# A hybrid decoder step on one core: sample queries computed ahead, pieces of the prompt redistributed over the groups, and a second buffer for transposed probabilities

## The chip, the cores and the metric

One core of one Trainium2 chip runs the kernel. The metric is the device time of one execution in microseconds. A core has these engines: TensorE (PE: matmuls and transposes by a matmul with the identity), VectorE (DVE), ScalarE (ACT), GpSimd (POOL) and SyncE (SP), which only issues DMAs. SP, ACT and POOL each issue DMAs in the order of their own program.

## The reference

The kernel computes one layer of a decoder for 512 prompt tokens and for 8 sequences of 8 sample tokens that have 4096 past positions each. Per group of tokens:

```python
qa, ka, va, qb, kb, vb = _project(_rms_norm(x, norm_attn_g[l]), w_in[l], pos)   # w_in is 1024 x 3072
oa = diff_attention(qa, ka, va, lam)       # 4 heads, 2 components of 64, values of 128; paged cache for the samples
ob = dilated_attention(qb, kb, vb)         # 8 heads of 64, windows 128/512/2048 with strides 1/4/16
x = x + _merge_heads(oa, ob, subln_g[l], w_out[l], lambda_init)
x = x + _swiglu(_rms_norm(x, norm_ffn_g[l]), w_gate[l], w_up[l], w_down[l])     # 2816 wide
```

A final norm follows. The samples' attention reads all past keys and values: 256 pages of 128 positions for the first kind of heads, and the last 2048 positions of each sequence for the second. The new keys and values, and the window buffers moved on by 8 positions, are outputs too. Everything is float32.

## The kernel before, in words

The kernel is written out by hand, one program per engine, with semaphores. Two things run interleaved: the prompt's work and the samples' attention.

**Groups.** The samples' attention is cut into 8 items (`QUADS`: four with 8 groups of pages, four with 3), 44 groups in all (`KSLOTS`). The main loop runs over `SLOTS` = 53 slots `t` with eight steps `i` each. In slot `t` the keys of group `t` are loaded (8 DMAs of 256 KB), transposed on VectorE (`turn_page`, L2280), multiplied with the samples' queries on TensorE (`score_keys`, L1305, half at step 2 and half at step 6) and moved out of PSUM with a running maximum (`keep_scores`, L2317). In the same slot the values of group `t - LAG` (`LAG` = 8) are weighed: `turn_probs` transposes the probabilities into PSUM bank X (L1318), ScalarE's `evac_probs` copies them to `pt_sb` (L1800, L1804), and `weigh_values` multiplies them with the values (L1342, L1359). The first 8 slots have keys alone, slots 8 to 43 keys and values, slots 44 to 52 values alone. `pt_sb` is one tile, so `evac_probs` waits until the group before has been weighed. In the last slots the values come from the samples' window state, and the DMAs for half of them are issued by ScalarE right behind `evac_probs`.

**Queries.** `fetch_q` and `fetch_first_q` lay an item's queries out for the scores. The first item needs the samples' columns of the first four tiles of the projection, after rotation (`rope`, L2154 to L2158).

**Pieces.** The prompt's work up to the feed-forward part is a list of 316 pieces: 192 of the projection (24 tiles of `w_in`, eight pieces a tile, six matmuls a piece, over all 576 columns, prompt and samples together), then prompt attention (32 units of one head and 128 queries, two pieces a unit), the output projection from piece 266 on, and the second norm of the prompt from piece 303 on. Each product of the projection is made of three fp32r matmuls: the weights and the activations are split into a high and a low part (`split_hi` on ScalarE L1594, `split` on GpSimd L1006, `norm_lo` on VectorE L2134). `SHARE` says how many pieces each slot takes; the 36 pieces of `PRE` run ahead of slot 0. Every engine goes through its part of each piece at the same place of its program, so the order is the same on all.

```python
PRE = 36
SHARE = [6] * 8 + [8] * 14 + [5] * 20 + [4, 4] + [3] * 4 + [0] * (SLOTS - 48)
```

**Start.** SP loads the prompt rows (blocks 0 to 3) and the sample rows (block 4), the gain, the first three tiles of `w_in` and constants, and then waits for the constants before it loads the first keys. The five blocks are normed in the order 0 to 4, transposed on TensorE (L1094) and split; the projection starts when all ten low halves are there. The move of the key window of sequence 0 (four DMAs of about 1 MB, `shift_window`, L780) runs beside the first tiles; the other moves run in the feed-forward part.

**End.** After slot 52 come the samples' output projection (`sample_out`, L1381), whose second half needs the last item's output, and the feed-forward part. Its gate and up products (L1410) and the down projection (L1477) keep TensorE busy to the end.

## Time and profile before

| | us |
|---|---|
| three runs | 1069.75, 1073.51, 1060.89; median 1069.75 |
| the profiled execution | 1071.72 |
| its span (first to last instruction) | 1070.0 |
| TensorE busy | 948.3 (89% of the span) |
| VectorE busy | 667.0 (62%) |
| ScalarE busy | 516.6 (48%) |
| GpSimd busy | 287.7 (27%) |
| DMA moved | 310.99 MB, 291 GB/s over the span |

The stages in the trace, with the end of a slot taken as the end of its `keep_scores`: norm of the input to 25.6 us; the 36 pieces ahead of the slots to about 60; slot 0 ends at 71.8, slot 7 at 126.3, slot 21 at 310.4, slot 23 at 334.9, slot 32 at 450.6, slot 35 at 484.4, slot 43 at 595.6; the values alone and the samples' output projection to 665.1; then the feed-forward part.

Busy time is not the bound by itself. A matmul's row in the trace lasts longer than the distance to the next row, since they are pipelined, and a busy share over the whole span mixes stages with different limits. The granted clock says how fast TensorE could run in a stretch; it has two levels, 1.2 and 2.4 GHz, shown as 0.5 and 1.0, and a stretch with both shows a number between them. DMA share is the mean busy share of 16 engines; a share of 1 or a little more means that they were always occupied.

### The profile page before, as it was taken

What the parts mean: (1) busy time and instruction counts of PE and PEld (TensorE: products, weight loads), DVE (VectorE), ACT (ScalarE), POOL (GpSimd) and SP (SyncE); (2) the same over time, 40 slices, a digit from 0 to 9 for tenths busy, and PEclk for the clock granted to TensorE, in tenths of its full rate; (3) what the DMA queues carried; (4) which work ended last, traced back from release to release, by engine and by line L of the source; (5) the groups of instructions that cost most, each with busy time, mean ns of one, the idle gap of its engine ahead of it and who ended that gap; (6) DMA issues with size and microseconds to landing.
All of it is one profiled execution on the core that took longest, in us unless ns stands there. A gap on an engine that the chain in (4) does not pass through costs nothing.

```text
span 1070.0 us, 29358 instructions
## 1 busy us (share of the span) xinstructions
PE 948.3 (89%) x11042; PEld 844.3 (79%) x11042; DVE 667.0 (62%) x1632; ACT 516.6 (48%) x1128; POOL 287.7 (27%) x351
## 2 busy tenths in 40 slices
PE   3989999899977888888898568899999999999996
PEld 2978888788855656676676444899999999999996
DVE  5289845676569997863546355888888888700004
ACT  6554433375236468664242653555555555611124
POOL 1322155555433355335454000000000000233330
PEclk8989999999999999998999868999999999999998
DMA  7789999999999999899988974487686876974632
GB/s 227 270 293 327 350 321 378 365 369 374 381 366 385 370 382 347 275 337 337 357 268 265 304 217 161 162 309 279 243 317 261 310 276 233 338 252 161 230 140 89
DMA packets 158229, 310.99 MB, mean 291 GB/s; under 512 B 14049, under 2 KB 88162, under 8 KB 157090
## 3 DMA queue, kind: packets, MB, share of 16 engines
q1 hardware_dynamic: 134242, 233.92, 63.0%
q0 software_dynamic: 22144, 72.37, 19.1%
q10 hardware_dynamic: 1728, 3.15, 0.9%
q8 instruction: 74, 1.21, 0.5%
q14 instruction: 41, 0.34, 0.1%
HBM read 302.31 MB, written 73.92 MB: 352 GB/s over the span
## 4 chain that ended last, share of the span: by engine, by line
PE 38%; issue 32%; DMA 15%; DVE 6%; ACT 5%; POOL 2%; POOLq 1%; ACTq 0%; SPq 0%; DVEq 0%
DMA v_ring<-in_cache_v_diff 12%; PE ps L1477 11%; PE ps L1111 9%; PE ps L1342 5%; PE ps L1305 4%; PE ps L1262 2%; DVE kt_sb L2280 1%; DMA v_ring<-in_state_v_win 1%; ACT rot L1616 1%; POOL v_ring L698 1%; PE ps L1318 1%; PE ps L1359 1%; PE ps L1188 1%; DMA x<-in_x_prompt 1%; DMA k_ring<-in_cache_k_diff 1%
## 5 line engine op out<-in xcount | busy, mean ns | idle before, releaser
L2280 DVE STREAM_TRANSPOSE kt_sb<-k_ring 128x512 f32<-128x512 f32 x336 | 218.7, 688 | 67.7 <-DMA k_ring<-in_cache_k_diff 30.7
L698 POOL DMA_DIRECT2D v_ring<-in_cache_v_diff x248 | 136.3, 551 | 157.6 <-issue 84.5
L1050 POOL TENSOR_TENSOR c_lo<-c_raw,c_hi 128x1408 fp32r<-128x1408 f32 x14 | 46.6, 3331 | 410.7 <-ACT c_hi L1893 410.7
L1111 PE MATMUL ps<-h_hi,w_hi 128*128 128x288 f32 x384 | 124.8, 325 | 1.9 <-DVE h_lo L2134 1.9
L1111 PE MATMUL ps<-h_lo,w_hi 128*128 128x288 f32 x384 | 115.8, 301 | 0.0
L1342 PE MATMUL ps<-v_ring,pt_sb 128*32 128x128 f32 x2240 | 79.2, 283 | 40.8 <-DMA v_ring<-in_cache_v_diff 34.0
L1111 PE MATMUL ps<-h_hi,w_lo 128*128 128x288 f32 x384 | 115.3, 300 | 0.0
L1342 PEld LDWEIGHTS ps<-v_ring,pt_sb 128*32 128x32 f32 x2240 | 61.1, 113 | 53.2 <-issue 49.5
L1305 PE MATMUL ps<-kt_sb,q_st 128*32 128x128 f32 (+1 forms) x2816 | 95.4, 278 | 6.2 <-DVE q_st L2290 4.1
L1006 POOL TENSOR_TENSOR w_lo<-w_raw,w_hi 128x1024 fp32r<-128x1024 f32 x24 | 57.4, 2392 | 153.7 <-ACT w_hi L1594 153.7
L1305 PEld LDWEIGHTS ps<-kt_sb,q_st 128*32 128x32 f32 x2816 | 72.0, 113 | 23.1 <-issue 16.2
L1111 PEld LDWEIGHTS ps<-h_hi,w_hi 128*128 128x128 f32 x384 | 74.5, 194 | 15.9 <-issue 13.6
L1477 PE MATMUL ps<-a_hi,c_hi 128*128 128x288 f32 x352 | 79.1, 296 | 0.2 <-POOL c_lo L1050 0.2
L1410 PE MATMUL ps<-t_h,s_h 128*128 128x288 f32 x264 | 77.9, 295 | 1.1 <-ACT u L1886 1.1
L1477 PE MATMUL ps<-a_lo,c_hi 128*128 128x288 f32 x352 | 78.9, 295 | 0.0
L1477 PE MATMUL ps<-a_hi,c_lo 128*128 128x288 f32 x352 | 78.5, 294 | 0.0
L1410 PE MATMUL ps<-t_l,s_h 128*128 128x288 f32 x264 | 77.9, 295 | 0.0
L1410 PE MATMUL ps<-t_h,s_l 128*128 128x288 f32 x264 | 77.7, 294 | 0.0
L2419 DVE TENSOR_TENSOR s_l<-s_t,s_h 128x512 fp32r<-128x512 f32 x88 | 58.7, 687 | 28.5 <-ACT s_h L1857 18.1
L1111 PEld LDWEIGHTS ps<-h_lo,w_hi 128*128 128x128 f32 x384 | 74.7, 195 | 0.0
L1111 PEld LDWEIGHTS ps<-h_hi,w_lo 128*128 128x128 f32 x384 | 74.6, 194 | 0.0
L2570 DVE TENSOR_TENSOR x<-x,ps 128x512 f32 x7 | 4.8, 686 | 111.1 <-PE ps L1490 111.1
(249 smaller groups left out, 2346.9 us busy)
## 6 DMA issues: line engine op xcount, KB each, us to landing
k_ring<-in_cache_k_diff SPq DMA_DIRECT2D x256, 256.0 KB, 7.1
v_ring<-in_cache_v_diff POOLq DMA_DIRECT2D x248, 256.0 KB, 7.0
out_k_win_sample<-in_state_k_win SPq DMA_DIRECT2D x32, 1020.0 KB, 8.2
out_v_win_sample<-in_state_v_win SPq DMA_DIRECT2D x32, 1020.0 KB, 8.2
k_ring<-in_state_k_win SPq DMA_DIRECT2D x32, 512.0 KB, 6.7
w_raw<-in_w_in SPq DMA_DIRECT2D x24, 512.0 KB, 7.3
g_raw<-in_w_gate SPq DMA_DIRECT2D x11, 1024.0 KB, 5.4
g_raw<-in_w_up SPq DMA_DIRECT2D x11, 1024.0 KB, 5.4
```

Source lines behind the costliest of these rows:

```text
L698: queue.dma_start(dst, src.rearrange("(b j) c -> j b c", b=4))\
L1006: nc.gpsimd.tensor_tensor(w_lo[:, n % 3, :], w_raw[:, n % 3, :], w_hi[:, n % 2, :].bitcast(F32), ALU.subtract).then_inc(w_lo_done, 1)
L1050: nc.gpsimd.tensor_tensor(c_lo[j][:, 0:width], c_raw[:, j, 0:width], c_hi[j][:, 0:width].bitcast(F32), ALU.subtract).then_inc(w_lo_done, 1)
L1111: last = nc.tensor.matmul(M[c][:, 0:HALF], wt, act[:, k, c * HALF:(c + 1) * HALF], start=k == 0 and at_first, stop=k == KT - 1 and act is ...
L1188: last = nc.tensor.matmul(Y[:, qb * P + 64 * c:qb * P + 64 * c + 64], weights_t, v_tok[:, kb, T * P + 64 * c:T * P + 64 * c + 64], start=k ...
L1262: last = nc.tensor.matmul(M[m % 2], wt, act[:, k, :], start=k == 0 and at_first, stop=k == KT - 1 and act is mix_h and not at_first)
L1305: last = nc.tensor.matmul(S[32 * f:32 * f + 32, c0:c0 + 32 * n], q_st[place_of(it)][:, h, f, r, :], kt_sb[:, 4 * h:4 * h + n, c:c + 32], s ...
L1342: last = nc.tensor.matmul(O[32 * f:32 * f + 32, P * h:P * h + P], pt_sb[:, 4 * f + b, :], values[:, f * P:(f + 1) * P], start=g == 0 and b ...
L1410: last = nc.tensor.matmul(ps[:, bank, 0:HALF], wt[:, k, :], act[:, k, :], start=j in (0, 1, 3) and k == 0 and at_first, stop=k == 3 and wt ...
L1477: last = nc.tensor.matmul(main_ps[:, 2 * bank + c, 0:HALF], wt[j][:, w], a_lo[:, pair, block, :] if low else a_hi[pair][:, block, :], star ...
L2280: V.transpose(kt_sb[:, i, :], k_ring[:, i, :]).then_inc(kt_done, 1)
L2419: V.tensor_tensor(dst[:, :, :], src, high[:, :, :].bitcast(F32), ALU.subtract).then_inc(form_low, 1)
```

## The change

1. **Samples' queries first.** The sample block is normed first (`NORM_ORDER`), and `project_samples` multiplies its transposed rows with the first four weight tiles in plain f32, straight from the raw weights, as soon as those land. `copy_sample_queries` and `rope_sample_queries` finish the first items' queries before the rest of the norm. The fourth weight tile has a place of its own (`early_raw`). The projection of tiles 0 to 3 then covers the 512 prompt columns alone. ScalarE issues the loads of the prompt rows, the first keys are loaded as soon as the page numbers are there, and the four moves of sequence 0's key window go to the down projection.
2. **All pieces in the groups.** `PRE` is 0. `SHARE` gives 9 pieces to each of slots 0 to 7, 8 to slots 8 to 21 as before, 6 or 5 (once 7) to slots 22 to 35, 5 and 5 to 36 and 37, and 4 to slots 38 to 47. The fourth item's queries are laid out in place 0 at the end of slot 23, where they came into place 1 in steps during it.
3. **Two places for transposed probabilities.** From slot 44 on `pt_sb` has two tiles, and from slot 45 on `turn_probs` and `evac_probs` of a slot run at step 5 of the slot before.

The core of the diff:

```diff
-    return 0 if it < 3 else it % 2
-
-
-FETCH_AT = {23: 3, 30: 4, 33: 5, 36: 6, 39: 7}
+    return 0 if it < 4 else (it + 1) % 2
+
+
+FETCH_AT = {30: 4, 33: 5, 36: 6, 39: 7}
...
-PRE = 36
+PRE = 0
...
-SHARE = [6] * 8 + [8] * 14 + [5] * 20 + [4, 4] + [3] * 4 + [0] * (SLOTS - 48)
+SHARE = ([9] * 8 + [8] * 14 + [6] * 4 + [5] + [6] * 5 + [7] + [5, 5, 6] + [5, 5] + [4] * 10
+         + [0] * (SLOTS - 48))
...
-            if i == 4 and has_v(t):
+            if i == 4 and has_v(t) and t <= KSLOTS:
                 out.append(("p", t))
+            if i == 5 and t >= KSLOTS and has_v(t + 1):
+                out.append(("p", t + 1))
...
+def prob_place(t):
+
+
+    return t % 2 if t >= KSLOTS else 0
...
+        pt_sb = [at("pt_sb0", [P, 16, 32], region(2048)), at("pt_sb1", [P, 16, 32], W0 + 28672)]
...
+        NORM_ORDER = (4, 0, 1, 2, 3)
...
+            return slice(256 * c, 256 * c + 256) if n < 4 else slice(c * HALF, (c + 1) * HALF)
...
-                if n >= 3:
+                if n >= 4:
                     sp.wait_ge(w_used, n - 2)
...
+            load_x(4)
+            sp.dma_start(g_rows[:, :], ins["norm_attn_g"].partition_broadcast(P)).then_inc(norm_in[0], 16)
+            sp.dma_start(ident[:, :], consts[:, C_ID:C_ID + P]).then_inc(norm_in[0], 16)
+            sp.dma_start(page_ids[:, :], ins["page_table"].rearrange("b n -> (b n)").unsqueeze(0)).then_inc(norm_in[0], 16)
+            for n in range(4):
+                w_in_chunk(n)
...
+            sp.wait_ge(norm_in[0], 48)
+            for i in range(8):
+                load_keys(0, i)
...
-
-            sp.wait_ge(const_in, 16 * N_CONST)
-            for i in range(8):
-                load_keys(0, i)
...
-                    if j == 0 and n and n + 2 < TILES:
+                    if j == 0 and n >= 2 and n + 2 < TILES:
...
-                    if j == 4 and n < COPIES:
-                        shift_window(*shifts.pop(0))
...
+                if m % 2:
+                    shift_window("k_win", 0, m // 2)
...
                 if j == 7:
                     last.then_inc(w_used, 1)
+
+            def project_samples(n):
+
+                pe.wait_ge(*landing_of(n))
+                pe.wait_ge(qs_copied, 2)
+                for k in range(KT):
+                    last = nc.tensor.matmul(Z[1][:, n * NS:n * NS + NS], raw_at(n)[:, k * P:k * P + P], h_s[:, k, :],
+                                            start=k == 0, stop=k == KT - 1)
+                last.then_inc(qs_projected, 1)
 
             def turn_tokens(n):
...
+            norm_transposes(0, NORM_ORDER[0])
+            for n in range(4):
+                project_samples(n)
+            for u in range(1, NBLK):
+                norm_transposes(u, NORM_ORDER[u])
             pe.wait_ge(hlo_done, 2 * NBLK)
-            for p in range(PRE):
-                main(p)
...
+            def copy_sample_queries():
+
+                act.wait_ge(qs_projected, 4)
+                cols = slice(0, 4 * NS)
+                nc.scalar.activation(feat[:, 1, cols], Z[1][:, cols], ACT.Copy).then_inc(qs_copied, 1)
+                act.wait_ge(qs_copied, 3)
+                for q in range(4):
+                    s = slice(32 * q, 32 * q + 32)
+                    d = slice(32 * (q ^ 1), 32 * (q ^ 1) + 32)
+                    last = nc.scalar.activation(rot[d, cols], feat[s, 1, cols], ACT.Copy)
+                last.then_inc(qs_copied, 1)
...
-                if q:
+                pt = pt_sb[prob_place(t)]
+                if t > KSLOTS:
+                    act.wait_ge(pv_half[1], q - 1)
+                    act.wait_ge(pv_half[0], q - 1)
+                elif q:
                     act.wait_ge(pv_half[1], q)
...
-                if t > KSLOTS and has_v(t + 2):
-                    place_state(act, q + 2, 1)
+                if t > KSLOTS + 1 and has_v(t + 1):
+                    place_state(act, q + 1, 1)
...
+                if u >= 2:
+                    act.wait_ge(sumsq_done, u - 1)
+                norm_stats(u, NORM_ORDER[u])
+
+            for blk in range(4):
+                act.dma_start(x[0:P, blk, :], x_of(blk)).then_inc(x_in[blk], 16)
+            squares_of(0)
+            norm_root(0, NORM_ORDER[0])
+            act.wait_ge(xn_t, 1)
+            for q in range(2):
+                nc.scalar.activation(h_s[:, 4 * q:4 * q + 4, :],
+                                     norm_bank(0, 4, q).rearrange("p (k c) -> p k c", k=4)[:, :, 0:NS], ACT.Copy)\
+                    .then_inc(qs_copied, 1)
+            norm_hi(0, NORM_ORDER[0], h_hi)
             split_hi(0)
-            for blk in range(NBLK):
-                norm_hi(blk, blk, h_hi)
+            squares_of(1)
+            norm_root(1, NORM_ORDER[1])
+            squares_of(2)
+            norm_root(2, NORM_ORDER[2])
+            copy_sample_queries()
+            squares_of(3)
+            norm_root(3, NORM_ORDER[3])
+            norm_hi(1, NORM_ORDER[1], h_hi)
+            fetch_q(0)
+            squares_of(4)
+            norm_root(4, NORM_ORDER[4])
+            norm_hi(2, NORM_ORDER[2], h_hi)
+            norm_hi(3, NORM_ORDER[3], h_hi)
+            norm_hi(4, NORM_ORDER[4], h_hi)
             act.wait_ge(lam_step, 2)
             nc.scalar.activation(lam_exp, lam_sum, ACT.Exp).then_inc(lam_e, 1)
-            for p in range(PRE):
-                main(p)
...
+            def rope_sample_queries():
+
+                dve.wait_ge(const_in, 16 * N_CONST)
+                dve.wait_ge(qs_copied, 4)
+                for f in range(4):
+                    s = slice(f * NS, f * NS + NS)
+                    V.tensor_tensor(feat[:, 1, s], feat[:, 1, s], rope_cs[:, 0, SEQ:NT], ALU.mult)
+                    last = V.tensor_tensor(rot[:, s], rot[:, s], rope_cs[:, 1, SEQ:NT], ALU.mult)
+                last.then_inc(rope_parts, 2)
+                dve.wait_ge(rope_parts, 2)
+                for f in range(4):
+                    s = slice(f * NS, f * NS + NS)
+                    V.tensor_tensor(q_s[:, f, :], feat[:, 1, s], rot[:, s], ALU.add).then_inc(rope_s_done, 1)
+
             def norm_blocks():
-                for blk in range(NBLK):
-                    norm_mean(blk, blk)
-                    if blk:
-                        norm_rows(blk - 1, blk - 1)
-                norm_lo(0, 0, h_hi, h_lo)
-                norm_rows(NBLK - 1, NBLK - 1)
-                for blk in range(1, NBLK):
-                    norm_lo(blk, blk, h_hi, h_lo)
+                def mean(u):
+                    norm_mean(u, NORM_ORDER[u])
+
+                def rows(u):
+                    norm_rows(u, NORM_ORDER[u])
+
+                def low(u):
+                    norm_lo(u, NORM_ORDER[u], h_hi, h_lo)
+
+                mean(0)
+                dve.wait_ge(norm_in[0], 48)
+                rows(0)
+                low(0)
+                mean(1)
+                rows(1)
+                mean(2)
+                rows(2)
+                rope_sample_queries()
+                fetch_first_q()
+                mean(3)
+                low(1)
+                rows(3)
+                mean(4)
+                low(2)
+                rows(4)
+                low(3)
+                low(4)
...
+                c = slice(0, SEQ if n < 4 else NT)
+                V.tensor_tensor(feat[:, n % 2, c], feat[:, n % 2, c], rope_cs[:, 0, c], ALU.mult).then_inc(rope_parts, 1)
+                V.tensor_tensor(rot[:, c], rot[:, c], rope_cs[:, 1, c], ALU.mult).then_inc(rope_parts, 1)
+                dve.wait_ge(rope_parts, 2 * no + 2)
+                if n >= 4:
+                    V.tensor_tensor(dst_s[:, T, :], feat[:, n % 2, SEQ:NT], rot[:, SEQ:NT], ALU.add).then_inc(rope_s_done, 1)
                 V.tensor_tensor(dst[:, T, :], feat[:, n % 2, 0:SEQ], rot[:, 0:SEQ], ALU.add).then_inc(rope_done, 1)
```

How the order moves, at three places. First VectorE in the norm of the input, before the change; `h_lo` are the low halves of the prompt and sample columns, `q_s` the rotated sample queries, `xn` the normed rows:

```order
L2134 TENSOR_TENSOR h_lo<-ps,h_hi 128x4x128 x2
L2107 RECIPROCAL small<-small 64x1
L2117 SCALAR_TENSOR_TENSOR xn<-x,small,g_rows 64x1024
L2134 TENSOR_TENSOR h_lo<-ps,h_hi 128x4x128 x6
L2134 TENSOR_TENSOR h_lo<-ps,h_hi 128x4x64 x2
L2481 TENSOR_TENSOR lam_prod<-lam_in 128x128
L2483 TENSOR_REDUCE small<-lam_prod 128x2
```

The same engine with the change, from the third block's rows on:

```order
L2221 TENSOR_TENSOR feat<-feat,rope_cs 128x64
L2222 TENSOR_TENSOR rot<-rot,rope_cs 128x64
L2227 TENSOR_TENSOR q_s<-feat,rot 128x64 x4
L2403 COPY q_st_125<-q_s 32x8x8 x8
L2180 TENSOR_SCALAR small<-small 128x1
L2212 TENSOR_TENSOR h_lo<-ps,h_hi 128x4x128 x2
L2185 RECIPROCAL small<-small 128x1
L2195 SCALAR_TENSOR_TENSOR xn<-x,small,g_rows 128x1024
```

The sample queries' rotation and the layout of the first item's queries (L2221 to L2403) now stand ahead of two blocks' rows and of all eight low halves of the prompt, for which the projection waits.

TensorE at its start, before the change; `ps` is PSUM, `h_hi` and `h_lo` the split activations:

```order
L1094 MATMUL ps<-ident,xn 128x128 x32
L1094 MATMUL ps<-ident,xn 128x64 x8
L1111 MATMUL ps<-h_hi,w_hi 128x288
L1111 MATMUL ps<-h_lo,w_hi 128x288
L1111 MATMUL ps<-h_hi,w_lo 128x288
```

And with the change:

```order
L1118 MATMUL ps<-ident,xn 128x64 x8
L1148 MATMUL ps<-h_s,w_raw 128x64 x24
L1148 MATMUL ps<-h_s,early_raw 128x64 x8
L1118 MATMUL ps<-ident,xn 128x128 x32
L1136 MATMUL ps<-h_hi,w_hi 128x256
```

The 32 plain f32 matmuls of the samples stand between the sample block's transposes and those of the prompt, and the first pieces of the projection have 256 columns where they had 288.

TensorE in slots 45 to 48, before the change; `t_ring`, `k_ring` and `v_ring` hold values here, and `ident,s_sb` are transposes of probabilities:

```order
L1373 MATMUL ps<-v_s,ptm 32x128 x8
L1094 MATMUL ps<-ident,xn_110 128x128 x8
L1318 MATMUL ps<-ident,s_sb 128x128 x4
L1342 MATMUL ps<-t_ring,pt_sb 32x128 x16
L1419 MATMUL ps<-ident,o_row 128x128
L1342 MATMUL ps<-t_ring,pt_sb 32x128 x16
L1094 MATMUL ps<-ident,xn_110 128x128 x8
L1318 MATMUL ps<-ident,s_sb 128x128 x4
L1342 MATMUL ps<-k_ring,pt_sb 32x128 x32
L1318 MATMUL ps<-ident,s_sb 128x128 x2
L1359 MATMUL ps<-v_ring,pt_sb 32x128 x32
L1326 MATMUL ps<-ident,s_sb 64x128
```

And with the change:

```order
L1407 MATMUL ps<-v_s,ptm 32x128 x8
L1118 MATMUL ps<-ident,xn_111 128x128 x8
L1352 MATMUL ps<-ident,s_sb 128x128 x4
L1376 MATMUL ps<-t_ring,pt_sb_67 32x128 x16
L1453 MATMUL ps<-ident,o_row 128x128
L1118 MATMUL ps<-ident,xn_111 128x128 x8
L1376 MATMUL ps<-t_ring,pt_sb_67 32x128 x16
L1118 MATMUL ps<-ident,xn_111 128x128 x8
L1352 MATMUL ps<-ident,s_sb 128x128 x2
L1376 MATMUL ps<-k_ring,pt_sb_68 32x128 x32
L1352 MATMUL ps<-ident,s_sb 128x128 x4
L1393 MATMUL ps<-v_ring,pt_sb_67 32x128 x32
```

The transposes of a slot's probabilities (L1318, now L1352) now stand ahead of the weighing of the slot before, and the `pt_sb` tiles alternate. The rest of the prompt's norm transposes (L1094, now L1118) still stands between them.

## Rows read from the trace of the kernel before

**Rows 1.** Windows: length, then PE, PEld, DVE, ACT, POOL busy us, clock, DMA share, GB/s.

```profile
0.00:25.60 25.60, 7.33 (x40) 6.61 (x40) 13.50 (x26) 15.49 (x29) 4.04 (x8) 0.91 0.78 222
25.60:60.00 34.40, 33.92 (x234) 33.68 (x234) 12.43 (x27) 20.04 (x32) 11.96 (x5) 0.91 0.75 258
60.00:71.80 11.80, 8.12 (x90) 7.41 (x91) 7.84 (x26) 6.74 (x16) 2.40 (x1) 0.71 0.91 315
71.80:126.30 54.50, 53.22 (x734) 47.98 (x733) 49.53 (x130) 22.08 (x39) 11.96 (x5) 1.00 1.03 341
126.30:310.40 184.10, 170.43 (x2578) 147.98 (x2579) 108.17 (x291) 82.78 (x180) 86.04 (x118) 0.98 1.03 364
334.90:450.60 115.70, 96.88 (x1607) 72.60 (x1608) 98.60 (x348) 76.12 (x234) 49.65 (x90) 0.99 0.98 350
484.40:595.60 111.20, 95.46 (x1338) 72.52 (x1333) 52.07 (x168) 34.65 (x107) 51.18 (x71) 0.92 0.96 308
595.60:665.10 69.50, 46.25 (x690) 31.22 (x689) 33.04 (x76) 40.50 (x75) 0.00 (x0) 0.78 0.67 199
665.10:1070.00 404.90, 391.13 (x2954) 389.66 (x2952) 245.07 (x384) 181.75 (x310) 46.63 (x14) 0.99 0.66 243
```

**Rows 2.** Timeline 23 to 66 us: start, duration, engine, operation [idle before].

```profile
23.47 4.57 SPq L830 DMA_DIRECT2D k_ring<-in_cache_k_diff  x8
25.63 0.61 PE L1111 MATMUL ps<-h_hi,w_hi 128*128 128x288 f32 x1 [1.88 <-DVE h_lo L2134]
60.18 2.11 ACT L1783 ACTIVATE q_st<-q_s 32x64 f32<-32x64 f32 x8 [1.45 <-DVE q_s L2157]
61.94 1.59 DVE L2290 COPY q_st<-q_s 32x64 f32<-32x64 f32 x8
...
63.67 1.93 PE L1305 MATMUL ps<-kt_sb,q_st 128*32 128x128 f32 x32 [4.13 <-DVE q_st L2290]
```

**Rows 3.** Timeline 69 to 72 us, TensorE: one half of a group, a piece.

```profile
69.68 1.08 PE L1305 MATMUL ps<-kt_sb,q_st 128*32 128x128 f32 x32
...
71.06 0.29 PE L1111 MATMUL ps<-h_hi,w_lo 128*128 128x288 f32 x1
71.19 0.29 PE L1111 MATMUL ps<-h_hi,w_hi 128*128 128x288 f32 x1
```

**Rows 4.** Groups by line and shape, 0 to 66 us: prices of the norm.

```profile
L2117 DVE SCALAR_TENSOR_TENSOR xn<-x,small,g_rows 128x1024 f32<-128x1024 f32 x4 | 5.1, 1284 | 1.0 <-PE ps L1094 0.9
L2134 DVE TENSOR_TENSOR h_lo<-ps,h_hi 128x512 fp32r<-128x512 f32 x8 | 5.0, 674 | 0.0
L1585 ACT ACTIVATE h_hi<-ps 128x512 fp32r<-128x512 f32 x8 | 4.1, 586 | 0.2 <-PE ps L1094 0.2
```

**Rows 5.** Groups by line, VectorE, 334.9 to 450.6 us: key transposes, masks.

```profile
L2280 DVE STREAM_TRANSPOSE kt_sb<-k_ring 128x512 f32<-128x512 f32 x73 | 47.9, 687 | 0.4 <-PE ps L1305 0.4
L2172 DVE CUSTOM_DVE_ANT_0 prob<-ps,p_mask 128x384 f32<-128x384 f32 (+3 forms) x44 | 19.8, 484 | 1.8 <-PE ps L1157 1.8
```

**Rows 6.** Timeline: two units of prompt attention one behind the other.

```profile
336.55 0.92 PE L1157 MATMUL ps<-kT,qT 64*128 64x384 f32 x4
340.10 1.13 PE L1157 MATMUL ps<-kT,qT 64*128 64x512 f32 x4 [0.47 <-DVE small L2172]
```

**Rows 7.** Waits, 595 to 665 us: us in total, times, longest.

```profile
PE ps L1342 <- ACT pt_sb L1800: 11.8, 4, 5.9
PE ps L1359 <- ACT pt_sb L1804: 5.4, 3, 3.1
PE ps L1373 <- ACT ptm L1817: 4.2, 3, 3.5
```

**Rows 8.** Timeline of ScalarE at 600 us: a table load and what follows.

```profile
600.62 1.28 ACT L1835 ACT_TABLE_LOAD   x1
601.91 0.51 ACT L1835 ACTIVATE s_sb<-s_sb,small 128x256 f32<-128x256 f32 x1
```

**Rows 9.** The page, sixth part: DMA issues, KB each, us to landing.

```profile
out_k_win_sample<-in_state_k_win SPq DMA_DIRECT2D x32, 1020.0 KB, 8.2
```

158 lines of the change are left out of this document (74 added, 84 removed).

## The prediction

> **What bounds the kernel now.** I read the windows by stage first, since the stages have different limits; there the reader is to compare TensorE's busy time with the length, and both with the DMA share. From 665.1 us on TensorE is busy 391 of 405 us, and nothing in the change touches that stage but four more copies. From 71.8 to 126.3 us (slots 1 to 7, keys alone) it is busy 53.2 of 54.5 us, so these slots are bound by TensorE, though the DMA share is 1.03. From 126.3 to 450.6 us the DMA engines are full (shares 1.03 and 0.98, 364 and 350 GB/s), and TensorE has room, little up to 310 (170.4 of 184.1) and more behind (96.9 of 115.7). In the last slots, 595.6 to 665.1 us, nothing is full: TensorE 46.3 of 69.5 us, ScalarE 40.5, DMA share 0.67, and the granted clock is 0.78 [rows 1]. A change can win only ahead of 665.1 us: at the start, in the slots bound by DMA by giving them more of the work, and at the end of the attention.
>
> Then the timelines at the edges of these stages. The first piece starts at 25.63 us, and behind the pieces of `PRE` TensorE waits 4.13 us for the first item's queries, which VectorE lays out until 63.5 us [rows 2]. In the last slots the waits name ScalarE's copies of transposed probabilities: 11.8, 5.4 and 4.2 us, 21.4 in all [rows 7].
>
> **The prices.** A projection matmul follows the one before after 0.13 us (71.06, 71.19), so a piece of six takes 0.79 us; half a group's scores take 1.08 us [rows 3]. Slots 1 to 7 take 54.5 / 7 = 7.8 us with six pieces each [rows 1].
>
> **The start, TensorE.** The samples come first, so the prompt's norm ends later. The first keys wait until 23.47 us for the constants [rows 2]; in the first 25.6 us the DMA engines move 222 GB/s at a share of 0.78 [rows 1]. The fourth weight tile (0.5 MB) now stands ahead of the constants, 2.4 us at that rate, less what the early issue of the prompt rows by ScalarE gives back: I take the constants at 24.5 us. The plain f32 matmuls are not in the trace. A lower bound is a projection's pitch, 0.13 us; an upper one comes from slot 0's score products, 1.93 us for 32 at half the clock [rows 2], so 0.06 each, times four since they run four side by side: 0.24 us. So 32 take 4 to 8 us, and all but the last tile's 1 to 2 us lie beside the landing of the weights. They and ScalarE's copies end before the constants do; this edit costs nothing as long as the constants are later. Then VectorE rotates the queries (12 short instructions at 1.59 / 8 = 0.2 us, 2.5 us) and lays them out (1.6 us): 28.6 us. Behind that stands a chain of two engines for the last blocks: high half of block 0 (2 x 0.59), ScalarE's layout of the queries (2.1 and two more of it, 2.6), squares of the last block (1.2), roots (0.7), high halves (1.2), low half (0.7), rows (1.3), transposes (1.1), high (1.2), low (0.7) [rows 2, 4]: 11.9 us. Squares are taken like the rows, which are as wide; roots as three short instructions, transposes as eight at 0.13 us. The first piece starts at about 40.5 us in place of 25.6, 15 us later.
>
> Against that stands what TensorE no longer does before the end of slot 7. From 25.6 to 126.3 us, 100.7 us, it did 84 pieces; now 72, 12 x 0.79 = 9.5 us less. Slot 0 from 60 on took 11.8 us at a granted clock of 0.71 for three pieces and the scores, which at full clock are 3 x 0.79 + 2.2 + 0.8 = 5.3; the wait and the slow clock behind it, 6.5 us, go. Tiles 0 to 3 have 256 columns for 288: up to 192 x 0.13 x 0.11 = 2.8 us, nothing if the weight loads set the pitch; I take 2.5. So slot 7 ends at 40.5 + 100.7 - 9.5 - 6.5 - 2.5 = 122.7 us, 4 us earlier (bounds 12 earlier and 4 later, for a start at 33 or 48 us). In slots 0 to 7 the nine pieces set the pace: 7.8 + 3 x 0.79 = 10.2 us each. VectorE's eight transposes (0.69) and a rotation lie beside them. What is late next is the second group's keys: SP loads eight pages of values ahead of them once the norm's transposes are done, which just fits into slot 0.
>
> **The copies.** Four moves of 1 MB leave the start, where they lay beside pieces bound by TensorE, for the down projection. Both places have room (shares of 0.75 and 0.66), and one takes 8.2 us [rows 1, 9]. I take nothing; if the weights of the down projection came late by them, 1 or 2 us.
>
> **The slots bound by DMA.** Slots 8 to 21 have the same pieces and bytes: nothing. The debt of 12 pieces is paid behind. Up to slot 23 the projection still runs (184 of 192 pieces done at the end of slot 21), and slots 24 to 32 take 52 pieces in place of 45 (250 pieces done for 251). These nine slots took 115.7 us, 12.9 each; VectorE was busy 98.6 us, of which key transposes 47.9 and masks 19.8 [rows 1, 5]. Less 47.9 and about 1.1 us a group for the scores' way out, its work for 45 pieces is some 40 us, 0.9 a piece; TensorE's, less 4 us a group for scores and values (estimated as twice 2 x 1.08), some 60, 1.3 a piece. Seven more make VectorE 105 and TensorE 106 of 115.7 us: they fit, on average. In the first of these slots, where a unit costs VectorE most, they fit less well, and the queries of the fourth item are now laid out in one lump (20 copies of 0.26 us, 5 us on ScalarE) between slots 23 and 24, with TensorE's scores behind. I take 3 us of loss; below, nothing; above, see the first rival.
>
> **The output projection.** Slots 38 to 41 have four pieces for five; the real work of the moved ones goes to 42 and 43, where TensorE had room (95.5 of 111.2 us busy over the eight slots [rows 1]). Four pieces of 1.3 us are 5 us; the DMA share of 0.96 lets me take 2.
>
> **The last slots.** With a probability copy made one slot ahead, TensorE finds it there. Of the 21.4 us of waits those in slot 44 and those for `ptm` stay in part, say 9; 12 go, and with them some time at the slow clock. But the copies stand on ScalarE in a row with the norm's squares and roots and the exponentials of the last item, 40.5 us of work, and the norm starts a little later, since three pieces more stand ahead of it. The order of the changed program has seven table loads there where nine stood; a load takes 1.28 us and the exponential starts 0.01 us behind it [rows 8], so 2.6 us go. The Trainium skill (ScalarE: Activation LUTs, What ACT_TABLE_LOAD costs) says that a switch costs 2.66 us, as a drain of 1.38 us belongs to it; by that two fewer would give 5.3 us. The row shows no such pause. I follow the rows: 10 us in all (bounds 3, the table loads alone, and 15). What is late next is the value DMAs, which ScalarE issues between its copies.
>
> **The sum.** 4 - 3 + 2 + 10 = 13 us. The profiled execution took 1071.7 us with a span of 1070.0; it would become 1058.7. It lies 2 us above the median of the three runs, 1069.75, so I predict 1057 us. The three runs differ by 12.6 us, and about 1% is what a measurement of this kernel tells from no change.
>
> The prompt rows now go through ScalarE's queue. The Trainium skill (DMA: Bandwidth & Descriptors, Issuing engines are not separate DMA queues) says that this saves only issue time, since all queues share the same engines. The share of 0.78 [rows 1] leaves a little room beside it; if the second queue filled it, the constants would land some 4 us earlier and the sum would be 17, by the rule it stays 13.
>
> **The rivals.**
> - *The debt isn't hidden.* Nothing in a slot bound by DMA is free if each piece ties three engines in order. Then the 12 pieces cost their own 9.5 us and some waits, 13 in place of 3, and the time is 1067. For it: TensorE waits for VectorE's masks within a unit (0.47 us [rows 6]). Against: 84% busy.
> - *The end is bound by ScalarE and the values.* The copies move, but ScalarE's row of work keeps the pace and only the table loads go: 3 us for 10, 1064. For it: 40.5 us busy, most of it in the first slots. Against: 21.4 us of waits that name just these copies [rows 7].
> - *Slower: units set the pace.* Two units follow each other after 3.55 us, and TensorE waited for the mask in between [rows 6]; a slot of 12.9 us has 2.5 units, 5.1 us each. If that, and not the DMA, is their pace, the 12 pieces are 6 units and 31 us in place of 3, less what slots 22 and 23 give back, say 4: 24 us more, 1081. It decides against the change when a unit takes over 4.3 us (12.9 / 3) in slots 24 to 32. Against it: DMA at a share of 0.98 there.
> - *Better than thought.* The norm chain overlaps more (start at 35 us), the debt is free and the end gives 14: 5 + 3 + 4 more, 1045.
>
> **How the numbers follow.** The forecast has 0.46, the debt 0.16, the end 0.14, slower 0.10, better 0.14. The forecast's own spread is 6 us to each side; some two thirds of it lie below 1059, the limit of 1%. Faster by over 1%: 0.30 of the forecast, 0.14, and a little of the rivals near it, 0.48. Slower: 0.10. Within 1%: 0.42. The range goes from 1044 to 1076: it takes in all but half of the best case and the slow one.
>
> **What would show it.** First piece at 38 to 43 us; slot 7 ends at 119 to 126; slots 1 to 7 of about 10.2 us with TensorE full; slot 23 ends some 4 us earlier than 334.9 and slot 32 some 1 us earlier than 450.6; the last slots take 58 to 62 us in place of 69.5, with a granted clock over 0.78, and the waits for `pt_sb` fall below 9 us. A first piece after 46 us, or slots 24 to 32 of more than 13.6 us on average, would make the prediction wrong.

## The result, and the profile after

The change made the kernel slower: 1094.99 us (median of four runs, 1093.27 to 1096.61) for 1068.8 (four runs, 1060.89 to 1073.51), a ratio of 1.0264 with a 95% interval of 1.0214 to 1.0314. The forecast was 1057, the range 1044 to 1076. The profiled execution has a span of 1094.8 us, the one before 1070.0.

The windows of the changed kernel by stage, cut where [rows 1] are cut (same columns: length, PE, PEld, DVE, ACT, POOL busy, clock, DMA share, GB/s):

```profile
0.00:25.60 25.60, 11.65 (x58) 11.52 (x58) 6.92 (x11) 8.55 (x16) 4.22 (x8) 1.00 0.96 297
25.60:50.00 24.40, 13.24 (x60) 12.04 (x60) 13.62 (x43) 13.59 (x32) 0.75 (x1) 0.71 0.13 43
...
131.20:322.30 191.10, 175.25 (x2601) 152.29 (x2601) 111.51 (x286) 84.41 (x179) 92.86 (x122) 0.97 0.99 345
322.30:345.30 23.00, 17.51 (x304) 14.33 (x302) 13.50 (x45) 4.87 (x13) 8.64 (x16) 1.00 1.04 386
345.30:479.40 134.10, 108.57 (x1639) 79.90 (x1641) 109.37 (x388) 85.93 (x271) 50.54 (x91) 0.94 0.88 313
479.40:516.50 37.10, 33.24 (x514) 27.45 (x513) 24.24 (x86) 25.02 (x71) 14.62 (x25) 0.91 0.93 301
516.50:624.60 108.10, 93.03 (x1358) 70.30 (x1362) 52.25 (x167) 33.67 (x106) 49.98 (x69) 0.95 0.97 312
```

Read by stage, the loss has three places. Slot 7 ends at 131.2 for 126.3 us, where the forecast had 122.7. Slots 8 to 21 take 191.1 for 184.1 us, where it had no change. Slots 24 to 32 take 134.1 for 115.7, where it had 3 us. Slots 36 to 43 gave 3.1 us and the end 4.3.

Over slots 24 to 32 the DMA share fell from 0.98 to 0.88, but that is again an average. Slots 24 to 29 and slot 32 before, then slots 24 to 29, 30, 31 and 32 of the changed kernel:

```profile
334.90:408.50 73.60, 60.60 (x1017) 44.29 (x1018) 65.95 (x230) 46.95 (x151) 31.73 (x58) 0.98 1.03 378
436.50:450.60 14.10, 11.98 (x195) 8.85 (x188) 12.64 (x47) 9.04 (x27) 4.38 (x8) 1.00 0.80 255
```

```profile
345.30:425.60 80.30, 64.91 (x1032) 46.70 (x1033) 71.71 (x250) 48.71 (x162) 32.44 (x59) 0.94 1.02 369
425.60:441.30 15.70, 11.96 (x185) 8.93 (x185) 9.84 (x38) 13.87 (x42) 6.56 (x13) 1.00 0.84 305
441.30:457.80 16.50, 13.38 (x209) 10.36 (x211) 12.51 (x46) 11.62 (x31) 4.42 (x9) 1.00 0.70 227
457.80:479.40 21.60, 18.32 (x224) 13.91 (x219) 15.30 (x59) 11.72 (x37) 7.12 (x13) 0.84 0.57 179
```

In slots 24 to 29 the DMA engines stay full; from slot 30 on they do not, and 11.7 of the 18.4 us are lost there (before, slots 30 and 31 had shares of 0.96 and 0.95). The row 25.6 to 50 is new: for 24 us the DMA engines did next to nothing (share 0.13), because the keys of the first group had landed by 27.5 us, and what SP loads behind them (eight pages of values, the second group's keys) waits for the last of the norm's transposes, which here come at 43.5.

The start, timeline of the changed kernel, for [rows 2]:

```profile
15.03 10.48 PE L1148 MATMUL ps<-h_s,w_raw 128*128 128x64 f32 x48 [0.84 <-ACT h_s L1967]
...
25.20 3.53 PEld L1148 LDWEIGHTS ps<-h_s,early_raw 128*128 128x128 f32 x16
25.30 3.62 PE L1148 MATMUL ps<-h_s,early_raw 128*128 128x64 f32 x16
...
33.11 1.59 DVE L2403 COPY q_st<-q_s 32x64 f32<-32x64 f32 x8
...
47.43 0.58 PE L1136 MATMUL ps<-h_hi,w_hi 128*128 128x256 f32 x1 [2.01 <-DVE h_lo L2212]
```

The first piece starts at 47.43 us, not 40.5. The 32 plain f32 matmuls of the samples stand in the trace as 64 rows with 64 weight loads and take 14.1 us, 0.44 each, where the forecast's upper bound was 0.24. They run at the lower clock, though the window above shows 1.00: the trace holds no clock record ahead of 32.65 us, and a stretch without a record is shown as 1.00. The rows tell it. Plain f32 products of the same form (128 x 128 weights, 64 columns) in slot 32 of the changed kernel, at a granted clock of 1.00, take 1.00 us for eight rows, which are four matmuls, so 0.25 each:

```profile
458.60 1.00 PE L1222 MATMUL ps<-v_tok,probT 128*128 128x64 f32 x8
```

Where the granted clock is at its lower level, 16 such rows take 3.51 us (452.79 in the trace of l_late2, shown below), 0.44 a matmul again.

The end, waits of TensorE from the end of slot 43 to the first gate product (624.6 to 689.8 us), for [rows 7]:

```profile
PE ps L1453 <- ACT pt_sb L1859: 4.1, 1, 4.1
PE ps L1118 <- DVE xn L2195: 3.2, 1, 3.2
PE ps L1407 <- ACT ptm L1876: 2.3, 2, 2.0
PE ps L1360 <- ACT pt_sb L1859: 2.1, 1, 2.1
PE ps L1352 <- ACT pt_sb L1859: 2.1, 1, 2.1
PE ps L1376 <- DMA k_ring<-in_state_v_win: 1.5, 1, 1.5
PE ps L1393 <- DMA v_ring<-in_state_v_win: 1.1, 1, 1.1
```

Waits for ScalarE's copies are 10.6 us for 21.4 [rows 7], so 10.8 went, as the forecast had it (12). Table loads are seven for nine. But waits for the norm and for values came in their place (5.8 us), the clock is 0.76, and the stretch is 65.2 us for 69.5.

### The profile page after: what moved, and what is told of

The parts are those of the page before. It is cut to its first block, busy times and chain, and to the rows that moved or that the text cites. A ratio compares the mean times of both kernels' runs of the same rounds, so it can differ in the third digit from the quotient of the medians.

```text
span 1094.8 us, 29510 instructions
## 1 busy us (share of the span) xinstructions
PE 968.0 (88%) x11106; PEld 860.9 (79%) x11106; DVE 674.7 (62%) x1640; ACT 515.2 (47%) x1133; POOL 289.0 (26%) x351
## 3 DMA queue, kind: packets, MB, share of 16 engines
q0 software_dynamic: 22144, 72.37, 18.7%
## 4 chain that ended last, share of the span: by engine, by line
PE 35%; issue 30%; DMA 15%; DVE 9%; ACT 6%; POOL 1%; SPq 1%; ACTq 0%; POOLq 0%; DVEq 0%
PE ps L1514 11%; PE ps L1136 7%; DMA v_ring<-in_cache_v_diff 7%; PE ps L1339 4%; DMA k_ring<-in_cache_k_diff 4%; PE ps L1376 4%; DVE kt_sb L2393 3%; DMA wo_sb<-in_w_out 2%; DMA w_raw<-in_w_in 2%; DVE prob L2285 2%; PE ps L1296 1%; PE ps L1148 1%; PE ps L1222 1%; ACT q_st L1838 1%; PE ps L1206 1%
## 5 line engine op out<-in xcount | busy, mean ns | idle before, releaser
L1136 PE MATMUL ps<-h_hi,w_hi 128*128 128x288 f32 (+1 forms) x384 | 124.3, 324 | 2.0 <-DVE h_lo L2212 2.0
L1136 PE MATMUL ps<-h_lo,w_hi 128*128 128x288 f32 (+1 forms) x384 | 114.7, 299 | 0.0
L1136 PE MATMUL ps<-h_hi,w_lo 128*128 128x288 f32 (+1 forms) x368 | 110.2, 299 | 0.0
L1376 PE MATMUL ps<-v_ring,pt_sb 128*32 128x128 f32 x2240 | 81.8, 290 | 29.0 <-DMA v_ring<-in_cache_v_diff 22.3
L1136 PEld LDWEIGHTS ps<-h_hi,w_lo 128*128 128x128 f32 x368 | 71.7, 195 | 0.0
```

What stands on the lines that cost most here:

```text
L1136: last = nc.tensor.matmul(M[c][:, 0:cols.stop - cols.start], wt, act[:, k, cols], start=k == 0 and at_first, stop=k == KT - 1 and act is h ...
L1376: last = nc.tensor.matmul(O[32 * f:32 * f + 32, P * h:P * h + P], pt_sb[prob_place(t)][:, 4 * f + b, :], values[:, f * P:(f + 1) * P], sta ...
```

## The experiments

The edits of tables are shown as the line of `SHARE` alone, without its last term of zeros. A name in the text is the kernel's label. "Without debt" means that 84 pieces are done by the end of slot 7, as before. All ratios are to the kernel before, timed beside each; they were taken at four different times, at which the median of the kernel before was 1067.6 to 1068.7.

### First: the debt and the end, each alone

**a_pre12**, the changed kernel without debt; each engine runs 12 pieces ahead of slot 0:

```diff
-PRE = 0
+PRE = 12
+SHARE = [9] * 8 + [8] * 14 + [5] * 20 + [4, 4] + [3] * 4
```

> The changed kernel, but 12 pieces run ahead of slot 0 and the table from slot 22 on is that of the kernel before, so the debt of 12 pieces is gone. Theory D (the debt is what costs behind slot 21: a unit of prompt attention more in a slot is not hidden by the DMAs): slot 7 ends 9.5 us later than in the changed kernel (12 x 0.79), about 140.7, slots 24 to 32 take about 116 us for 134.1, slots 33 to 35 about 34, and the time is 1095 + 9.5 - 21 = about 1084. Rival S (the later start itself, with DMA engines idle from 25.6 to 50 us, is carried on into the later slots): slots 24 to 32 stay above 130 us and the time is about 1104.

**b_debt**, the kernel before with the debt alone:

```diff
-SHARE = [6] * 8 + [8] * 14 + [5] * 20 + [4, 4] + [3] * 4
+SHARE = [4, 5] * 4 + [8] * 14 + [6] * 4 + [5] + [6] * 5 + [7] + [5, 5, 6] + [5, 5] + [4] * 10
```

> The kernel before, with 4 or 5 pieces (36 in all) in slots 0 to 7 for 48, and the changed kernel's table from slot 8 on: the debt alone, without anything else of the change. Theory D: slot 7 ends 9.5 us earlier than 126.3, about 117, slots 24 to 32 take 131 to 134 us for 115.7, and the time is 1069 - 9.5 + 20 = about 1079. Rival S: the debt is hidden, slots 24 to 32 take at most 119 us, and the time is about 1062.

**c_oldtail**, the changed kernel with one `pt_sb` and the transposes at step 4 in all slots, and **d_newtail**, the kernel before with two. The edit as d_newtail has it, in part; c_oldtail takes it back:

```diff
-            if i == 4 and has_v(t):
+            if i == 4 and has_v(t) and t <= KSLOTS:
                 out.append(("p", t))
+            if i == 5 and t >= KSLOTS and has_v(t + 1):
+                out.append(("p", t + 1))
```

> The changed kernel with one place for copied probabilities and the old order at the end. The stretch from the end of slot 43 to the first gate product took 69.5 us before and 65.2 after. If the two places are what gives 4.3 us, it goes back to about 69.5 and the time is 1099. If the whole 10 us of the forecast are there but are hidden by the four pieces a slot that now stand in slots 44 to 47, it takes 75 us and the time is 1105. If the place gives nothing, 1095.

> The kernel before with the changed end alone (two places, one slot ahead). By the 4.3 us seen: 1065. By the forecast's 10 us: 1059. If the gain hung on the other order of pieces: 1069, no change.

Measured: a_pre12 1075.77 us (1.0063, 1.0032 to 1.0094); b_debt 1101.34 (1.0305, 1.0263 to 1.0347); c_oldtail 1097.59 (1.0254, 1.0217 to 1.029); d_newtail 1065.03 (0.996, 0.9924 to 0.9996). In a_pre12 slot 7 ends at 135.8 us (expected 140.7) and slots 24 to 32 take 114.5, so theory D had the place right and rival S is out; the time came 8 us under the expected 1084, and 5 of these are the 12 pieces, which cost 4.6 us by slot 7 and not 9.5. In b_debt slots 24 to 32 take 134.4 us, as theory D had it, but the time is 22 us over its 1079: slot 7 ends at 121.2 us for the 117 expected, and slots 8 to 21 take 190.8 us for 184.1. These and the rest make 21 us in the profiled execution, the fastest of its four (1093.09; the others are 1098 to 1105). By the median the debt alone costs 33 us, more than the whole change, and where the other 12 us go isn't known. The changed end is worth some 2.6 us by the median either way, with intervals of 3 to 4 us to each side; in the traces the stretch from slot 43 to the first gate product is 63.1 us in d_newtail for 69.5, and in c_oldtail 68.7 for 65.2, which is the first of its three cases.

### Second: where the debt is paid, and the start alone

**f_start**: the changed kernel with `PRE` = 36 and the table before. **g_early**: without debt, none ahead of slot 0. **i_pay**: the debt paid outside slots 28 to 32. **k_phase**: the kernel before with the tile's boundaries moved.

```diff
 f_start  SHARE = [6] * 8 + [8] * 14 + [5] * 20 + [4, 4] + [3] * 4
 g_early  SHARE = [10, 11] * 4 + [8] * 14 + [5] * 20 + [4, 4] + [3] * 4
 i_pay    SHARE = [9] * 8 + [8] * 14 + [6] * 6 + [5] * 5 + [5] * 11 + [4] * 4
 k_phase  SHARE = [6, 5] * 4 + [8] * 14 + [7, 7] + [5] * 18 + [4, 4] + [3] * 4
```

> The changed kernel with the 36 pieces ahead of slot 0 and the table of the kernel before: its start (samples first, fourth weight tile early, copies in the down projection) and its end, with no debt at all. Theory: the 36 pieces start some 22 us later than 25.63 (first piece at 47.4) and the wait for the queries (4.13 us) and the clock behind it go, so slot 7 ends at about 126 + 22 - 6.5 - 2.5 = 139; the rest as before, less 2.6 us at the end: 1077. Rival: the later start is made up in the slots bound by the DMA engines, since keys and values lie in their rings already: 1067.

> The kernel before with 44 for 48 pieces in slots 0 to 7 and the four paid in slots 22 and 23 (7, 7 for 5, 5). By slot 8 the count is 80, so each slot of 8 pieces is one whole tile, as in the changed kernel (72), where before it lay half a tile off (84). Theory P (the 7 to 8 us that the changed kernel loses in slots 14 to 21 come from where the tile's boundary falls in a slot): slots 14 to 21 take about 110 us in place of 103, slots 14 and 16 are the long ones, and the time is 1068 - 3 + 7 + 1 = about 1073. Rival (it comes from the later start of the values or from the size of the debt): 103 us there, and about 1066.

> The changed kernel with its debt of 12 pieces paid elsewhere: six of them in slots 22 to 27, none in slots 28 to 32 (five pieces each, for 6, 6, 6, 6, 7), six from slot 33 on. Theory C (slots 28 to 32 are those where the DMA engines aren't full any more and each unit more costs its own 5 us): slots 28 to 32 take 66 us for 80, slots 33 to 43 some 5 us more, and the time is about 1085. Rival (the cost follows the pieces wherever they stand): slots 28 to 32 gain, but the others lose as much, and it stays at 1095.

> The changed kernel without the debt in another way: none ahead of slot 0, but 10 or 11 pieces in each of slots 0 to 7, then the table of the kernel before. Theory: 12 pieces at 0.79 us more by slot 7, the rest as without the debt: like the run with 12 pieces ahead, 1076. If pieces in these slots are cheaper than ahead of them, since VectorE's and the DMA engines' work lies beside them: 1070; if the slots of 11 pieces let the DMA engines fall behind: 1080.

Measured: f_start 1081.85 us (1.0124, 1.0062 to 1.0187); g_early 1077.55 (1.0082, 1.0052 to 1.0112); i_pay 1084.29 (1.0135, 1.0076 to 1.0194); k_phase 1074.7 (1.0068, 1.0029 to 1.0107). The start costs more than expected: slot 7 of f_start ends at 144.2, for 139 expected. The wait ahead of slot 0's scores did go, but one slot later TensorE waits 4.39 us, behind VectorE, which sat 5.43 us idle until the second group's keys landed:

```profile
76.62 1.08 PE L1340 MATMUL ps<-kt_sb,q_st 128*32 128x128 f32 x32
84.59 2.72 DVE L2398 STREAM_TRANSPOSE kt_sb<-k_ring 128x512 f32<-128x512 f32 x4 [5.43 <-DMA k_ring<-in_cache_k_diff]
88.28 1.77 PE L1340 MATMUL ps<-kt_sb,q_st 128*32 128x128 f32 x32 [4.39 <-DVE small L2435]
```

i_pay has theory C's time, in part by luck: slots 28 to 32 take 69.6 us for 80.1 (66 expected), slots 24 to 27 cost 3.5 more, and 4.6 us come from slots 8 to 21, whose program is that of the changed kernel. g_early came out at theory's 1076 and k_phase at its 1073, each within 2 us. k_phase is 6 us slower than before with four pieces moved; in its trace slot 16 takes 18.9 us for 14.0, slots 14 to 21 take 104.4, of the 110 expected only a part (the profiled execution was the fastest of its ten).

### Third: copies, a credit, the f32 matmuls, the phase in the changed kernel

**e_copies** is d_newtail with the four copies moved; **l_late2** is e_copies with one piece less in slots 31 and 32 and one more in 44 and 45; **m_short** and **j_mix** come from the changed kernel, and m_short leaves out 28 of the 32 plain f32 matmuls.

```diff
 l_late2  SHARE = [6] * 8 + [8] * 14 + [5] * 9 + [4, 4] + [5] * 9 + [4, 4] + [4, 4] + [3] * 2
 j_mix    SHARE = [9, 10] * 4 + [8] * 14 + [6] * 6 + [5] * 5 + [5] * 9 + [4, 4] + [4, 4, 3, 3]
 m_short
-                for k in range(KT):
+                for k in (0,):
...
-                                            start=k == 0, stop=k == KT - 1)
+                                            start=True, stop=True)
```

> The kernel before with the changed end and the four copies of 1 MB in the down projection. Theory: slots 1 to 7 are bound by TensorE with or without the copies, and the down projection has room: the same as with the changed end alone, 1065. Rival: the copies crowded the keys' queue at the start (slots 3, 4 and 7 differed by up to 2 us between two executions of the same code), and without them slot 7 ends 4 us earlier: 1061.

> As the kernel with the changed end and the copies moved, and slots 31 and 32 have four pieces for five, slots 44 and 45 four for three: a credit where the changed kernel took a debt. Theory C (a unit costs some 5 us in slots 28 to 32): slots 31 and 32 take 23 to 24 us for 27.8, held up by the DMA share of 0.95 and 0.80 at which they stand, the last slots 1 us more: 3 us less than the other kernel of this call, about 1062. Rival (pieces are dearer in the last slots): no change or 2 us more.

> The changed kernel with 4 of the 32 plain f32 matmuls of the samples (the first of eight steps of each tile), so the samples' queries of the first item leave out seven eighths of their sum; it shows what these matmuls cost at the start. They took 14.1 us in the trace, 0.44 each. Theory: the fourth tile lands at 25.2 us whatever they take, so only its own 3.1 us go, the transposes of the prompt's blocks start at about 25.6 for 28.7, the first piece at 44 for 47.4, and the time is 1095 - 3 = 1092. Rival (their 14 us are the delay): first piece at 36 and 1084.

> The changed kernel with 76 pieces by slot 7 (9, 10), so that a tile's boundary falls in the middle of a slot again, and 28 to 32 left at five pieces each as in the run that paid elsewhere; four pieces less of debt. Theory P (the boundary of a tile at the boundary of a slot costs some 7 us in slots 14 to 21): 103 us there; 1084 + 3 at the start - 5 - 2 = about 1080. Rival (the later start or the debt itself): 106 to 111 us there and about 1087.

Measured: e_copies 1064.33 us (0.9959, 0.9927 to 0.9992), beside 1065.03 of d_newtail, so the copies cost and give nothing that these runs can tell. m_short 1087.95 (1.0163, 1.0107 to 1.022), first piece at 38.82: the f32 matmuls delayed it by 8.6 us and the end by 7, nearer to the rival. Theory had the landing of the fourth tile wrong: it lands at 18.83 us, and its matmuls waited for those ahead of them. j_mix: slots 14 to 21 take 103.2 us as theory P had it, and its trace has no wait of TensorE for ScalarE there. Its time settles nothing: the four runs are 1082.87 (the profiled one), 1092.26, 1100.12 and 1100.41, a median of 1096.19 (1.0267, 1.0208 to 1.0325) where 1080 was expected; the two lower ones have a mean of 1087.6, which is the rival's figure. Why this kernel's runs spread so is open.

l_late2 took theory C down: with a piece less in each of the two slots it is 1077.8 us (1.0076, 1.0047 to 1.0105), 13 us slower than e_copies. Windows of slots 31 to 33, first e_copies, then l_late2:

```profile
424.10:437.80 13.70, 11.29 (x201) 9.30 (x203) 10.44 (x43) 8.89 (x27) 6.76 (x12) 1.00 0.93 327
437.80:451.90 14.10, 11.98 (x195) 8.85 (x188) 12.64 (x47) 9.04 (x27) 4.38 (x8) 1.00 0.81 254
451.90:464.20 12.30, 11.94 (x185) 9.74 (x188) 8.06 (x36) 10.55 (x35) 4.38 (x8) 1.00 1.02 297
```

```profile
426.00:442.40 16.40, 12.14 (x181) 9.34 (x184) 9.61 (x39) 6.92 (x21) 6.76 (x12) 0.79 0.81 288
442.40:462.90 20.50, 16.13 (x199) 12.15 (x192) 12.42 (x45) 8.19 (x26) 4.38 (x8) 0.75 0.62 193
462.90:478.50 15.60, 12.60 (x186) 10.05 (x187) 8.33 (x36) 12.37 (x38) 4.38 (x8) 0.89 0.71 212
```

These are nearly the times of the changed kernel, whose slots 31 and 32 take 16.5 and 21.6 us, with six and seven pieces where l_late2 has four and four and the kernel before five and five. In l_late2 the clock says that TensorE ran slow, and the timeline says after what:

```profile
433.80 0.88 PE L1178 MATMUL ps<-ident,prob 128*128 128x128 f32 x3 [2.74 <-DVE small L2316]
434.47 1.81 PE L1194 MATMUL ps<-v_tok,probT 128*128 128x64 f32 x8
436.21 1.94 PE L1348 MATMUL ps<-v_ring,pt_sb 128*32 128x128 f32 x32
...
444.53 0.61 PE L1211 MATMUL ps<-ident,oT 128*128 128x128 f32 x4
...
451.69 1.09 PE L1324 MATMUL ps<-ident,s_sb 128*128 128x128 f32 x4 [3.58 <-DVE mix_l L2272]
452.57 0.42 PE L1178 MATMUL ps<-ident,prob 128*128 128x128 f32 x1
452.79 3.51 PE L1194 MATMUL ps<-v_tok,probT 128*128 128x64 f32 x16
...
456.23 1.94 PE L1348 MATMUL ps<-v_ring,pt_sb 128*32 128x128 f32 x32
```

At 444.53 the piece that ends a head puts its output transposes into a bank that mix_l on VectorE must have read; the group's probabilities (L1324) need it at step 4, and wait 3.58 us. Behind the wait the values' products take 1.94 us for the 1.08 of full clock. In e_copies the same transposes of a head come at 449.31, behind the probabilities, and nothing waits. The changed kernel has the same kind of wait in its slot 32, shorter, and one for VectorE's row in slot 31. There the clock stays at 1.00, so slot 31 is not long for the reason that it has in l_late2:

```profile
452.89 0.41 PE L1206 MATMUL ps<-ident,prob 128*128 128x128 f32 x2 [2.17 <-DVE small L2415]
460.99 0.70 PE L1191 MATMUL ps<-kT,qT 64*128 64x256 f32 x4 [1.38 <-DVE small L2285]
468.46 0.63 PE L1352 MATMUL ps<-ident,s_sb 128*128 128x128 f32 x4 [1.90 <-DVE mix_l L2371]
```

### Fourth: the place of a piece against the samples' steps

**p_swap** moves one piece of e_copies by one slot; **u_xearly** is l_late2 with the transposes of slot 32 one step later, on TensorE and ScalarE; **r_best** is e_copies with a debt of one whole tile, paid before slot 24.

```diff
 p_swap   SHARE = [6] * 8 + [8] * 14 + [5] * 9 + [4, 6] + [5] * 9 + [4, 4] + [3] * 4
 r_best   SHARE = [5] * 8 + [8] * 12 + [10] * 2 + [7] * 2 + [5] * 18 + [4, 4] + [3] * 4
 u_xearly
-            if i == 4 and has_v(t) and t <= KSLOTS:
+            if i == (5 if t == 32 else 4) and has_v(t) and t <= KSLOTS:
```

> The kernel before with the changed end and the copies moved, and one single piece moved by one slot: slot 31 has four, slot 32 six, all others as before. Theory X (what costs is not how many pieces a slot has, but which of them stands next to the steps of the samples' work there: the item ends in slot 31, and bank X and VectorE's row of work are shared): slots 31 and 32 take 33 us or more for 27.8, the clock falls to half behind the waits, and the time is about 1070. Rival (the count decides): 28 us for both, no change, 1064.

> The kernel of l_late2 (1078), with the probabilities' transposes and their copy in slot 32 alone at step 5 in place of 4, so behind the products of the piece that stood behind them. Theory X: the wait of 3.6 us for bank X (released by VectorE's mix_l) is filled by those products, the half clock behind it goes in part, slot 32 takes 15 to 17 us for 20.5, and the time is about 1074. Rival (VectorE's and ScalarE's chain sets the pace there, TensorE's wait is only where it shows): slot 32 stays above 19 us, 1078.

> The kernel before with the changed end, the copies moved, and a debt of eight pieces, one whole tile, in slots 0 to 7 (five each) that is paid in slots 20 to 23 (10, 10, 7, 7 for 8, 8, 5, 5), ahead of the prompt's attention proper; everything from slot 24 on as before. Theory X with DMA as the bound: the phase of the tiles is kept, the eight pieces lie beside the DMAs, slot 7 ends 6.3 us earlier, slots 20 to 23 take at most 4 us more: 1064 - 6 + 3 = 1061. Rival (no piece is hidden in a slot bound by DMA): they cost their own 6.3 us there and more, 1066.

Measured: p_swap 1068.16 us (0.999, 0.9965 to 1.0016), 4 us over e_copies, with 30.7 us in slots 31 and 32 for 27.8: theory X in sign, at half its size. Its slot 31 has l_late2's four pieces and the same wait of 2.74 us, but a granted clock of 0.89 for 0.79, and takes 15.1 us for 16.4. u_xearly 1075.61 (1.0062, 1.0037 to 1.0088): slot 32 takes 16.9 us for 20.5, the wait for `mix_l` there is 1.59 us for 3.58, and the end comes 2 us earlier, as theory X had it, less than the slot gives. So this wait is the cause of most of slot 32's loss; slots 33 to 35 take 41 us in both kernels, for 33.5 in e_copies, and that part of l_late2's 13 us isn't explained. Its waits, TensorE's rows of slots 31 and 32:

```profile
430.12 0.87 PE L1178 MATMUL ps<-ident,prob 128*128 128x128 f32 x3 [2.74 <-DVE small L2316]
...
448.08 0.63 PE L1324 MATMUL ps<-ident,s_sb 128*128 128x128 f32 x4 [1.59 <-DVE mix_l L2272]
```

r_best 1062.54 (0.9962, 0.9933 to 0.9991): faster than the changed kernel, and 0.4% under the kernel before, which is within 1%. Slot 7 ends at 123.2 us, and slots 24 to 32 take 113.9, as in e_copies (114.0). It isn't told apart from e_copies (2 us, with runs of both from 1059 to 1072).

### What the traces say together

Each number is the length of a stretch in one profiled execution, in us.

| slots | before | b_debt | after | i_pay | k_phase | j_mix | f_start | g_early | r_best |
|---|---|---|---|---|---|---|---|---|---|
| 0 to 7 (end) | 126.3 | 121.2 | 131.2 | 131.1 | 125.3 | 130.1 | 144.2 | 136.0 | 123.2 |
| 14 to 21 | 102.8 | 110.0 | 111.2 | 106.1 | 104.4 | 103.2 | 102.2 | 102.0 | 107.1 |
| 24 to 27 | 50.2 | 54.4 | 54.0 | 57.5 | 51.4 | 54.5 | 52.1 | 53.4 | 51.0 |
| 28 to 32 | 65.5 | 79.9 | 80.1 | 69.6 | 63.3 | 71.0 | 62.9 | 61.8 | 62.9 |
| 33 to 35 | 33.8 | 34.4 | 37.1 | 39.5 | 33.4 | 39.7 | 35.2 | 34.9 | 33.1 |

Every kernel whose count at slot 24 is that of before (k_phase, f_start, g_early, r_best) has the times of before from there on, within 4 us a row, and so do a_pre12, d_newtail and e_copies; slots 31 and 32 take 13.7 and 14.1 us in all of them. With the changed kernel's table they take 16.5 to 16.6 and 21.4 to 21.6 in after, b_debt, c_oldtail and m_short. Other rows are less steady: slot 7 of d_newtail ends at 130.6 with the program of before up to there, and slots 14 to 21 take 103.0 in d_newtail and 106.0 in e_copies with the same pieces, so such a row of one trace is good to some 4 us.

By medians the change comes apart in four steps: the end and the copies (before to e_copies, 1068.6 to 1064.3) -4.3; the samples first (to f_start, 1081.9) +17.5; all pieces in slots, without debt (to g_early, 1077.6) -4.3; the debt (to the changed kernel, 1095.0) +17.4. The sum is 26.3, as it must be. Medians of four runs are good to some 4 to 7 us here, and the debt costs 33 us where the rest of the change is absent (b_debt), so the last step isn't a price that holds by itself.

## Why the prediction was wrong

**The start (+6 forecast, +17.5 measured).** The forecast was 15 for the later first piece, less 6.5 for the wait and the clock, less 2.5 for the columns. The step that failed is the price of a plain f32 matmul: 0.44 us for the 0.13 to 0.24 taken as bounds. The lower bound is the pitch of an fp32r matmul. The upper one divides 1.93 us by 32 matmuls, but `score_keys` issues 16 for those 32 rows, since each plain f32 matmul has two. With that it is 0.48 us at the lower clock, and 0.44 lies under it; 0.25 is the price at full clock, which a TensorE that had done eight transposes in 15 us did not get. With 4 to 8 us for all 32 they would have ended before the constants; they ended at 28.9, while the constants had all landed by 22.2. m_short measures it: 8.6 us at the first piece. The chain behind the queries' layout was right (12.7 us from 34.7 to 47.4, for 11.9). The wait ahead of slot 0's scores went, but in f_start the second group's keys, which the forecast names as "late next" and prices at nothing, cost 4.4 us and a stretch at half clock one slot later. With that, slot 7 of f_start ends 18 us later than before, for a first piece 21.5 us later.

**ScalarE's queue for the prompt rows.** The constants landed at 22.2 us, 2.3 ahead of my 24.5, of the 4 that a second queue might give. But the DMA engines had no room to fill. In the first 18.7 us the share is 0.96 at 271 GB/s before and 0.97 at 287 now; the 0.78 of [rows 1] comes from the time behind, in which little was on its way but the rest of the constants. The 297 GB/s over 25.6 us hold 1.9 MB more than before, and these are in the main the fourth weight tile and the first keys, issued at 18.96 us for 23.47. This agrees with the rule of the Trainium skill (DMA: Bandwidth & Descriptors, Issuing engines are not separate DMA queues) that a second issuing engine saves only issue time. It bought nothing here in any case, since TensorE was late.

**The copies** cost nothing, as forecast (e_copies beside d_newtail: 1064.33 and 1065.03; the last stage of the changed kernel takes 405.0 us for 404.9).

**The debt (-8.5 forecast: 9.5 won at the start, 3 and -2 behind; +17.4 measured).** The step that failed is "they fit, on average", the 3 us for what lies behind slot 21. It and its neighbours have four parts.
- The gain at the start was half: 12 pieces fewer by slot 7 gave 4.6 us (a_pre12 to the changed kernel), 4.8 (g_early) and 5.1 (b_debt), 0.4 us a piece for the 0.79 taken. I had called slots 1 to 7 bound by TensorE, with a DMA share of 1.03 beside it; in b_debt they take 7.3 us each with 4.6 pieces on average, for 7.8 with six.
- The sum itself was short: the changed table has 54 pieces in slots 24 to 32, not 52, so nine more and not seven. In slots 24 to 30 six pieces more go with 8.1 us more (96.0 for 87.9), 1.35 us a piece, near the 1.3 that the forecast had as TensorE's price and hid behind the DMAs. That the pieces' own work costs it is not shown. In slots 24 to 29 the DMA share is 1.02, as full as before, and 29.6 MB are moved for 27.8, which at 369 GB/s is 4.9 of the 6.7 us there: work that slots 8 to 21 had left behind, with 65.9 MB for 67.0. Against that, b_debt takes 80.7 us there with 28.7 MB.
- The place of the pieces was not in the sum at all. Slots 31 and 32 take 10.3 us more with three pieces more, where the share before was 0.95 and 0.80 and not the 0.98 of the nine slots, and l_late2 has 9.1 us more with two pieces fewer. So the number of pieces alone does not decide; u_xearly shows that in l_late2 it is the piece beside the probabilities' transposes. That the changed kernel's 10.3 us have this cause is argued from the same kind of wait in slot 32 (1.90 us), and was not tested there; its three pieces more would be 4 us of it at the forecast's 1.3.
- Slots 8 to 21 have "the same pieces and bytes: nothing" in the forecast, and took 7 us in this trace. Number and bytes were the same, but with 72 done at slot 8 each slot is one whole tile, and a tile's first step (the split of new weights on ScalarE, which waits for their DMA) stands ahead of the exponentials and the copy of probabilities. The changed kernel in slots 14 and 16:

```profile
216.59 1.06 ACT L1631 ACTIVATE w_hi<-w_raw 128x1024 fp32r<-128x1024 f32 x1 [9.05 <-DMA w_raw<-in_w_in]
...
220.46 0.60 ACT L1859 ACTIVATE pt_sb<-ps 128x512 f32<-128x512 f32 x1
...
221.11 1.93 PE L1376 MATMUL ps<-v_ring,pt_sb 128*32 128x128 f32 x32 [5.80 <-ACT pt_sb L1859]
...
244.47 1.06 ACT L1631 ACTIVATE w_hi<-w_raw 128x1024 fp32r<-128x1024 f32 x1
...
246.96 0.72 ACT L1894 ACTIVATE s_sb<-s_sb,small 128x512 f32<-128x512 f32 x1
...
249.94 0.66 PE L1352 MATMUL ps<-ident,s_sb 128*128 128x128 f32 x4 [3.74 <-ACT s_sb L1894]
```

In slot 16 of the kernel before, the exponentials (`s_sb`) come ahead of the split, and TensorE does not wait for them:

```profile
236.28 0.72 ACT L1835 ACTIVATE s_sb<-s_sb,small 128x512 f32<-128x512 f32 x1
...
240.75 1.06 ACT L1594 ACTIVATE w_hi<-w_raw 128x1024 fp32r<-128x1024 f32 x1
```

The wait of 3.7 us for `s_sb` in slot 16 is in all six traces with whole tiles (after, b_debt, c_oldtail, i_pay, k_phase, m_short), and in none of the eleven with half a tile. The wait for `pt_sb` in slot 14 is not a matter of order alone: it is 5.8 us here, 3.1 to 5.2 in b_debt, c_oldtail and m_short, and under 1 us in i_pay and k_phase, since it hangs on when a weight tile lands. So the phase costs the 3.7 us, and sometimes the second wait; slots 8 to 21 take 185.2 to 191.1 us in the six traces and 181.4 to 187.0 in the ten others that have the same pieces there (before 184.1).

The rival "units set the pace" had the right place, sign and nearly the size (24 us), and stood at 0.10. Its mechanism, a price of 5.1 us a unit, is not what the runs show: 8.1 us for three units in slots 24 to 30, and in slots 31 and 32 a time that depends on which pieces stand there, not on how many alone.

**The output projection** (2 us forecast) gave 3.1 in the trace, which says little: slots 36 to 43 take 106.5 to 112.5 us in kernels with the pieces of before there.

**The end (-10 forecast, some -3 measured).** The waits for ScalarE's copies went nearly as forecast (10.8 of 12 us). The step that failed is that waits which go shorten the stage by as much: 5.8 us of waits for the norm and for values came in their place, the clock stayed at 0.76, and 46.7 us of TensorE's work and 38.1 of ScalarE's, with the norm between the two, fill most of the 65.2. The 2.6 us for two table loads were wrong too. The loads go with the table of pieces and not with the two places: b_debt has seven and takes 69.7 us for this stretch, d_newtail has nine and takes 63.1. So the second rival ("bound by ScalarE and the values", 3 us) had the size by the median, but not its reason, the table loads alone. In the traces the stretch is 61.1 to 66.2 us with the changed end and 65.4 to 69.7 without.

## What to carry to other kernels

Where several engines walk one order written out by hand, a piece moved by a slot is a new program at every place behind it: a slot with fewer pieces can be the slower one. Move whole periods (here a tile of eight pieces) and be back at the old count before the part where waits are tight; r_best does that and loses nothing, though it isn't shown to gain. Read the DMA share slot by slot before calling a piece free. Price a matmul by the rows of its own kind and at the clock of its place, and count rows against the program, since one matmul can have two.

## What was new of the hardware here

A plain f32 matmul of 64 columns with 128 x 128 weights stands in the trace as two weight loads and two products. It takes 0.25 us at a granted clock of 1.00 (458.60 in the changed kernel) and 0.44 at the lower level of 1.2 GHz (452.79 in l_late2, and the samples' 32); an fp32r one of 288 columns takes 0.13 at full clock [rows 3].

A wait of TensorE can cost more than itself. Behind 2.74 and 3.58 us the granted clock was 0.79 and 0.75 over the two slots of l_late2, its lower level for some 7 and 10 us (twice 0.21 of 16.4 and twice 0.25 of 20.5), in which products that take 1.08 us took 1.94. But it need not. In the same trace a wait of 3.10 us for values ends at 202.63, after projection pieces without a gap, and the 32 rows behind it take 1.08 us at a clock of 1.00; and behind the same 2.74 us p_swap had 0.89 over the slot where l_late2 had 0.79. So the length of a wait alone does not say what the clock will do.
